# A decoder layer with 64 experts: a third buffer for the experts' gate and up weights, all weights on one queue

## What is computed

```python
gprob = jax.nn.softmax((hf @ w_rg) + b_rg, axis=-1)          # top 1 of 8 groups
elog = ...                                                    # top 2 of the group's 8 experts
def expert_block(args):
    xi, e = args
    return (jax.nn.silu(xi @ w_gate[e]) * (xi @ w_up[e])) @ w_down[e]
yb = lax.map(expert_block, (xb, block_expert)).reshape(R, D)
y = jax.ops.segment_sum(yb * slot_w[:, None], slot_tok, num_segments=T + 1)[:T]
```

## Time and profile before

| | |
|---|---|
| median of 3 runs | 1601.09 us (1597.41 to 1610.74) |
| the profiled execution's own time | 1600.42 us |
| its span, first to last instruction | 1598.7 us |
| TensorE busy | 1375.1 us (86%), granted clock 0.933 of full speed in the mean |
| VectorE, ScalarE, GpSimd busy | 827.9, 332.8, 245.4 us |
| moved by DMA | 277.85 MB, 174 GB/s in the mean |
| chain that ended last | PE 48%, DMA 21% (w_up alone 18%), DVE 19% |

### The profile page before, as it was taken

The page is one execution under the profiler, slowest core; times in us unless marked ns, Lnnn a source line. Parts: engine busy times, 40 slices in busy tenths (PEclk is TensorE's granted clock), DMA queues, the critical chain, the costliest instruction groups (busy, mean ns, idle before and its releaser), DMA issues.

```text
span 1598.7 us, 20949 instructions
## 1 busy us (share of the span) xinstructions
PE 1375.1 (86%) x6824; PEld 786.0 (49%) x6824; DVE 827.9 (52%) x1742; ACT 332.8 (21%) x901; POOL 245.4 (15%) x356
## 2 busy tenths in 40 slices
PE   5899999999999899999999698777887788877881
PEld 4548557575585665855847564532332232322330
DVE  1296685875857848668587323462223222222225
ACT  3123223232222322212323211101111111111112
POOL 2211121111210211012111100014111111111110
PEclk9999999999999999999999779778999899998996
DMA  8921030311202202103020440259999999999994
GB/s 193 162 54 41 28 94 2 80 40 28 69 25 61 61 25 56 40 28 94 0 54 19 169 131 40 101 232 405 414 416 402 418 403 397 413 398 414 386 372 185
DMA packets 126884, 277.85 MB, mean 174 GB/s; under 512 B 21500, under 2 KB 95158, under 8 KB 102134
## 3 DMA queue, kind: packets, MB, share of 16 engines
q1 hardware_dynamic: 103990, 196.21, 34.0%
q10 hardware_dynamic: 10704, 66.06, 11.3%
q0 software_dynamic: 12160, 15.19, 3.0%
HBM read 272.43 MB, written 30.62 MB: 190 GB/s over the span
## 4 chain that ended last, share of the span: by engine, by line
PE 48%; DMA 21%; DVE 19%; issue 7%; ACT 5%; ACTq 0%; DVEq 0%; SPq 0%; POOLq 0%; POOL 0%
DMA arena<-in_w_up 18%; PE PB L1505 10%; PE PB L1161 7%; DVE arena L1679 5%; PE PB L1155 5%; DVE arena L1651 4%; PE PB L1111 4%; PE PB L1429 4%; PE PB L1239 2%; PE PB L1267 2%; DMA arena<-in_w_gate 1%; PE PB L1132 1%; PE PB L1088 1%; PE PB L1361 1%; PE PB L1322 1%
## 5 line engine op out<-in xcount | busy, mean ns | idle before, releaser
L1505 PE MATMUL PB<-arena 128*64 128x512 f32 x1024 | 263.5, 663 | 79.9 <-DMA arena<-in_w_up 67.7
L1505 PEld LDWEIGHTS PB<-arena 128*64 128x64 f32 x1024 | 76.5, 151 | 239.4 <-issue 145.9
L2023 DVE TENSOR_SCALAR arena<-arena 128x256 f32<-128x256 f32 x32 | 9.4, 294 | 327.5 <-ACT arena L996 327.4
L1155 PE MATMUL PB<-arena 128*128 128x384 f32 x512 | 171.2, 488 | 6.5 <-DVE arena L1652 6.5
L1161 PE MATMUL PB<-arena 128*128 128x128 f32 x1280 | 167.6, 286 | 6.2 <-ACT arena L874 5.5
L1137 PE MATMUL PB<-arena 128*128 128x512 f32 x384 | 169.1, 596 | 0.0
L1161 PEld LDWEIGHTS PB<-arena 128*128 128x128 f32 x1280 | 157.0, 199 | 14.2 <-ACT arena L874 7.4
L935 ACT ACTIVATE arena<-PB 128x512 f32<-128x512 f32 (+3 forms) x116 | 60.0, 521 | 384.7 <-PE PB L1513 211.5
L1155 PEld LDWEIGHTS PB<-arena 128*128 128x128 f32 x512 | 95.4, 190 | 70.8 <-DVE arena L1652 7.6
L1525 PE MATMUL PB<-arena 128*64 128x512 f32 x512 | 118.4, 605 | 12.1 <-DMA arena<-in_w_down 11.6
L1137 PEld LDWEIGHTS PB<-arena 128*128 128x128 f32 x384 | 71.6, 190 | 88.0 <-issue 87.5
(11 more groups left out here) (436 smaller groups left out, 1991.5 us busy)
## 6 DMA issues: line engine op xcount, KB each, us to landing
arena<-in_w_gate SPq DMA_DIRECT2D x64, 1024.0 KB, 11.0
arena<-in_w_down SPq DMA_DIRECT2D x64, 1024.0 KB, 19.5
arena<-in_w_up ACTq DMA_DIRECT2D x60, 1024.0 KB, 13.9
arena<-in_w_in SPq DMA_DIRECT2D x58, 512.0 KB, 6.2
Sb<-in_state_dn SPq DMA_DIRECT2D x8, 512.0 KB, 4.1
out<-Sb POOLq DMA_DIRECT2D x8, 512.0 KB, 3.9
arena<-in_w_out SPq DMA_DIRECT2D x1, 4096.0 KB, 12.2
arena<-in_w_up SPq DMA_DIRECT2D x4, 1024.0 KB, 7.5
```

The lines of the kernel that those rows point to most:

```text
L1155: last = mm(gate_bank[(n + 1) % 2][0:R, 0:3 * P], hT[:, c, n * P:n * P + R], wrow[:, c, :, :].rearrange("p g k -> p (g k)"), start=c == 0, ...
L1505: last = mm(gu_bank[a][half[k], :], xT[:, a, c, half[k]], wgu[a][:, k, :, c, :], start=c == 0, stop=c == KC - 1)
```

## The change

Gate and up weights of a pair get a third buffer, `wgu2`, and pair j uses buffer j mod 3. To make room the arena grows by 1792 elements a partition, `wgu1` begins right behind ys instead of behind xr, and hb and hid (the silu's tiles) move into pT and sig, which only the mixer uses. `wgu2` lies over router scratch (rt, M and others), so its first load waits for `s_ov_done`; both buffers of down weights now end below it, in the place of the router's h2T, and are both loaded after `s_lg_ps`. All expert weights, the ups too, are asked for by SP. Since 2 and 3 buffers meet again after six pairs, the loops of SP and TensorE go over six pairs. The two semaphores of the result copies, s_ye_a and s_ye_v, become one, s_ye_done. The diff, cut:

```diff
-        wgu_at = 37632 - 2 * KC * 2 * FE
+        wgu_at = 39424 - 2 * KC * 2 * FE
         X = cut(2, D)
         xT = cut(2, KC, P)
-        hb = cut(2, FE)
-        hid = cut(2, FE)
+        hb = pT.rearrange("p (a b) k -> p a (b k)", a=2)
+        hid = sig.rearrange("p a g k -> p (a g k)")[:, 0:2 * FE].rearrange("p (a f) -> p a f", a=2)
         hidT = cut(2, FE // P, P)
         ys = cut(2, D)
         assert top[0] <= xr_end
-        top[0] = xr_end
         wgu1 = cut(2, 2, KC, FE)
         wdn = (cut(2, FE // P, D), cut(2, FE // P, D))
+        assert top[0] <= h2_end
+        wgu2 = cut(2, 2, KC, FE)
         assert top[0] <= wgu_at
         top[0] = wgu_at
-        wgu = (cut(2, 2, KC, FE), wgu1)
+        wgu = (cut(2, 2, KC, FE), wgu1, wgu2)
...
+        def pair6(it, r):
+            return it * 6 + r, it * 3 + r // 2, r % 2, it * 2 + r // 3, r % 3
+        def later6(it, r, k):
+            return pair6(it + (r + k) // 6, (r + k) % 6)
...
@@ block.sync
-            sp.wait_ge(s_y2_ps, NT)
+            sp.wait_ge(s_x2_done, NT)
             for k in range(2):
                 load_gate_up(1, k, 2 + k)
             sp.wait_ge(s_lg_ps, NT)
+            for a in range(2):
+                for k in range(2):
+                    load_down(a, k, 2 * a + k)
+            sp.dma_start(nfin, norm_final_w.partition_broadcast(P)).then_inc(s_fin_in, 16)
+            sp.wait_ge(s_ov_done, 1)
             for k in range(2):
-                load_down(0, k, k)
-            sp.dma_start(nfin, norm_final_w.partition_broadcast(P)).then_inc(s_fin_in, 16)
-            def gate_up_weights(it, a):
-                sp.wait_ge(s_gu_ps, 1 + it * 2 + a)
+                load_gate_up(2, k, 4 + k)
+            def gate_up_weights(it, r):
+                j, _, _, _, g = pair6(it, r)
+                sp.wait_ge(s_gu_ps, j)
                 for k in range(2):
-                    sp.dma_start(wgu[a][:, k, 0, :, :], w_gate[...]).then_inc(gu_in[a], 16)
-            def down_weights(it, a):
-                sp.wait_ge(s_dn_ps, 1 + it * 2 + a)
+                    load_gate_up(g, k, j * 2 + k)
+            def down_weights(it, r):
+                j, _, a, _, _ = pair6(it, r)
+                sp.wait_ge(s_dn_ps, 1 + j)
                 for k in range(2):
-                    load_down(a, k, it * 4 + (2 * a + k))
-            with sp.Fori(1, NPAIR // 2) as it:
-                gate_up_weights(it, 0)
-                sp.wait_ge(s_ov_done, 1)
-                down_weights(it - 1, 1)
-                gate_up_weights(it, 1)
-                down_weights(it, 0)
-            down_weights(NPAIR // 2 - 1, 1)
+                    load_down(a, k, j * 2 + k)
+            gate_up_weights(0, 3)
+            for r in range(2, 6):
+                gate_up_weights((r + 2) // 6, (r + 2) % 6)
+                down_weights(0, r)
+            with sp.Fori(1, NPAIR // 6) as it:
+                for r in range(6):
+                    gate_up_weights(it + (r + 2) // 6, (r + 2) % 6)
+                    down_weights(it, r)
+            for r in range(NPAIR % 6):
+                down_weights(NPAIR // 6, r)
...
@@ block.scalar
-            def up_weights(it, a):
-                j = it * 2 + a
-                act.wait_ge(s_gu_ps, 1 + j)
-                for k in range(2):
-                    act.dma_start(wgu[a][:, k, 1, :, :], w_up[...]).then_inc(gu_in[a], 16)
...
@@ block.tensor
             def gate_up(p, c0, c1):
+                j, _, a, i, g = p
                 if c0 == 0:
                     pe.wait_ge(s_xt_done, 1 + j * 2 + 2)
-                    pe.wait_ge(gu_in[a], it * 64 + 64)
+                    pe.wait_ge(gu_in[g], i * 64 + 64)
                 for c in range(c0, c1):
                     for k in range(2):
-                        last = mm(gu_bank[a][half[k], :], xT[:, a, c, half[k]], wgu[a][:, k, :, c, :], ...)
+                        last = mm(gu_bank[a][half[k], :], xT[:, a, c, half[k]], wgu[g][:, k, :, c, :], ...)
-            with pe.Fori(0, NPAIR // 2 - 1) as it:
-                for a in range(2):
-                    overlapped(it, a)
-            overlapped(NPAIR // 2 - 1, 0, turn=False)
+            with pe.Fori(0, NPAIR // 6) as it:
+                for r in range(6):
+                    overlapped(it, r)
+            overlapped(NPAIR // 6, 0, turn=False)
```

More of the change, by code:

```diff
@@ L211, in program @@
         h2T = cut(2, KC, P)
+        h2_end = top[0]
         brb = cut(72)
@@ L1032, in _ @@
                 follow(0, a)
-            with act.Fori(1, NPAIR // 2 - 2) as it:
+            with act.Fori(1, NPAIR // 2 - 1) as it:
                 for a in range(2):
                     follow(it, a)
[L1036 to L1039, removed]
+            follow(NPAIR // 2 - 1, 0, turn=False)
+            follow(NPAIR // 2 - 1, 1, nxt=False, turn=False)
             def further(it, a, k):
@@ L1496, in turn_x, with gate_up, turn_hid @@
                     last.then_inc(s_xt_ps, 1)
-            def gate_up(it, a, c0, c1):
-                j = it * 2 + a
+            def gate_up(p, c0, c1):
+                j, _, a, i, g = p
                 if c0 == 0:
                     pe.wait_ge(s_xt_done, 1 + j * 2 + 2)
-                    pe.wait_ge(gu_in[a], it * 64 + 64)
+                    pe.wait_ge(gu_in[g], i * 64 + 64)
                 for c in range(c0, c1):
                     for k in range(2):
-                        last = mm(gu_bank[a][half[k], :], xT[:, a, c, half[k]], wgu[a][:, k, :, c, :], start=c == 0, stop=c == KC - 1)
+                        last = mm(gu_bank[a][half[k], :], xT[:, a, c, half[k]], wgu[g][:, k, :, c, :], start=c == 0, stop=c == KC - 1)
                 if c1 == KC:
                     last.then_inc(s_gu_ps, 1)
-            def turn_hid(it, a):
-                j = it * 2 + a
+            def turn_hid(p):
+                j, _, a, _, _ = p
                 pe.wait_ge(s_hid_done, j + 1)
@@ L1514, in turn_hid, with down @@
                 last.then_inc(s_hT2_ps, 1)
-            def down(it, a):
-                j = it * 2 + a
+            def down(p):
+                j, i, a, _, _ = p
                 pe.wait_ge(s_hT2_done, j + 1)
-                pe.wait_ge(dn_in[a], it * 32 + 32)
-                pe.wait_ge(s_ye_a, 1 + j)
-                pe.wait_ge(s_ye_v, 1 + j)
+                pe.wait_ge(dn_in[a], i * 32 + 32)
+                pe.wait_ge(s_ye_done, 2 + 2 * j)
                 for q in range(2):
@@ L1527, in down, with overlapped @@
                 last.then_inc(s_dn_ps, 1)
[L1530 to L1533, removed]
+            def overlapped(it, r, turn=True):
+                gate_up(later6(it, r, 1), 0, KC // 2)
+                turn_hid(pair6(it, r))
+                gate_up(later6(it, r, 1), KC // 2, KC)
                 if turn:
[L1535 to L1540, removed]
-            with pe.Fori(0, NPAIR // 2 - 1) as it:
-                for a in range(2):
-                    overlapped(it, a)
-            overlapped(NPAIR // 2 - 1, 0, turn=False)
-            turn_hid(NPAIR // 2 - 1, 1)
-            down(NPAIR // 2 - 1, 1)
-            def further(it, a, k):
-                turn_x(it, a)
-                gate_up(it, a, 0, KC)
-                turn_hid(it, a)
-                down(it, a)
+                    turn_x(later6(it, r, 2))
+                down(pair6(it, r))
+            turn_x(pair6(0, 0))
+            gate_up(pair6(0, 0), 0, KC)
+            turn_x(pair6(0, 1))
+            with pe.Fori(0, NPAIR // 6) as it:
+                for r in range(6):
+                    overlapped(it, r)
+            overlapped(NPAIR // 6, 0, turn=False)
+            turn_hid(pair6(NPAIR // 6, 1))
+            down(pair6(NPAIR // 6, 1))
+            def further(it, a, k):
+                p = pair2(it, a)
+                turn_x(p)
+                gate_up(p, 0, KC)
+                turn_hid(p)
+                down(p)
             further_blocks(pe, further)
```

34 lines of the change are left out of this document (15 added, 19 removed).

## The result

The changed kernel takes 1621.8 us (median of 4 runs, 1617.9 to 1629.2) where the kernel before took 1602.2 beside it: a ratio of 1.012, 95% interval 1.009 to 1.015. It is slower by 1.2%, and outside the predicted range. Its profiled execution took 1617.9 us, with a span of 1616.1.

A forecast was written before the change was run, and what follows sets the result against it. The expert-pair stage was taken as bound by the bytes; the twelve microseconds gained from the dips were spent at the start (7.1 and 5.0), TensorE ending 0.5 us earlier, so about 1600 us, range 1588 to 1612.

The forecast's parts named there:

- the dips: Expert-pair loop: bandwidth dips are a queue run dry, a third buffer fills them; gain 10.6 us and another 1.5 or so.
- No window under 400 until 1540: Sign for the expert-pair stream: after the idle start, no bandwidth window under 400 GB/s until 1540.
- (B): Rival, expert-pair stream: dips not a dry queue or prefetch not real; mean rate stays 407, 11.2 us more, 1611; chance 0.18.
- The start: First pairs' loads: unmoved bytes put the stream 7.1 us behind at ov_done (overflow table done), itself 5.0 us later.
- The stream: Weight loads from 1084.8 to pair 29's down: 191.7 MB at 417 GB/s, 459.8 us, plus 1.2 and 0.9.
- the release: SP's wait for ov_done ahead of pair 2's gate and up loads: ends at 1083.2 instead of 1078.2.
- the sum: Whole kernel: span 1598.2, plus 1.7 for the profiled run and 0.7 for the median, 1600.6, say 1600.
- The tail: From the start of down 29: TensorE needs 19.2 us as before, no new wait; the 32.3 us behind untouched.
- what costs nothing: Side edits: ScalarE loses two DMA issues a pair (0.8 us), SP issues six loads, merged semaphore, moved tiles, unrolled loop: free.
- (C): Rival, SP's queue: one queue with POOL's rows carries less than two; at 402 GB/s 17.1 us more, 1618; chance 0.07.
- (D): Rival, stream and start: one queue carries 424 GB/s with rows, gather not held up; 7.7 and 5.0 less, 1588; chance 0.18.

The follow-up runs named there:

- e1: The changed kernel with indices out of bounds for 28 of 32 pairs' gathers and scatters, so their rows don't move: 1592.3 us, ratio 0.991.
- e2: The changed kernel with each expert's token rows spread over other partitions by a table of places, same bytes: 1609.5 us, ratio 1.003.
- e3: The kernel before, with its two buffers, and the token rows spread over other partitions by a table of places: 1592.7 us, ratio 0.991.
- e8: The changed kernel with each expert's token rows crowded on fewer partition groups, same bytes: 1671.4 us, ratio 1.041.
- e6: The changed kernel with only pair 1's down loads moved back behind pair 0's gate and up products: 1623.3 us, ratio 1.011.
- e4: The changed kernel with pair 2's gate and up loaded into pair 0's buffer, then pair 1's down, before the wait for ov_done: 1606.4 us, ratio 1.001.
- e5: The kernel before, two buffers and its own start, with the up weights also issued from SP's queue: 1608.0 us, ratio 1.003.

## Why the prediction was wrong

**The step that failed is "the dips".** It said that they are a queue run dry, that a third buffer should fill them, and that the stream then has 417 GB/s up to its end. They fell on the issue times, and SP's queue was in fact short of work there. But by e1, e2, e3, e8 and the increments TensorE waited for the slowest engine's share of a load, and for that engine the stream had no break. The queue ran dry for the engines that were ahead. The deeper queue was real, and it filled: the rate of 1100 to 1300 is its filling, 419 GB/s where the kernel before had 410, and none of it shortened a wait. "No window under 400 until 1540" held until 1315 (395) and broke for good from 1380. The forecast had 12.1 us gained there; from down 5 to down 29, 2.3 were lost.

What spoke against it stood in the prediction itself: at a DMA share of 0.76 in a dip most engines are busy, which a queue run dry doesn't explain. Rival (B) named it ("not all is idle there") and asked no further which engines were busy and with what.

**The start was sized nearly right.** ov_done came 4.9 us later, the prediction had 5.0, and e6 takes it back. In part that is luck: the 5.0 were for the gather alone, which lost 3.6 (nearer to the 3.3 that the prediction set beside its own number), and the other 1.3 were lost before and behind it. The bytes that hadn't moved were put at 7.1; together 12.1, measured 14.1 by down 5. At 16.31 us for the 6.29 MB of a pair, 3.0 MB are 7.8 us and not 7.1; the other 1.4 us are not settled. Since the dips gave nothing back, all of it stood: e4 shows that it is the loss but for 0.6 us.

**The stream** was to take 461.9 us from 1084.8 to down 29; it took 478.9 from 1085.9 (the issue at 1084.3 and the 1.6 to the first bytes). Counted the other way: 184.5 MB of weights are 29.3 pairs, at the measured 16.31 us 478. Of the 18.1 us by which down 29 came later than forecast, 17.0 are this term, mis-sized because it took the mean rate for the rate of a load; the other 1.1 are the release, in a run whose mixer ended 1.2 us later. The median lies 3.9 us above the profiled execution, where the sum had 0.7.

**The tail and what costs nothing** held. Down 29 to the end of down 31 took 19.3 us (19.2 forecast), and 32 us stood behind it. The two issues less on ScalarE, the six loads on SP and the unrolled loop show in no wait.

**The rivals.** (B) gave 1611 by its mean rate of 407, the nearest in kind: the dips were not cured. Its price was short, because it took the mean of the engines again. The time came out where (C) had put it, 1618 and more, but (C)'s mechanism is refuted: one queue keeps the pace within 0.04 us of two (e5), and the kernel after showed 418 to 420 with the rows in it. (D), 424, fell with it.

## What to carry to other kernels

A bandwidth that dips is not always for want of buffers, and a dip at the issue times is no proof of it: compare the time that a unit of work takes with the bytes of the busiest engine, not with the mean over 16, and see how far apart a load's 16 increments lie. Small rows that are gathered and scattered beside a stream cost by the engine on which they crowd; choose their partitions so that each engine gets the same number. And an edit that puts an early load behind a late semaphore can cost its full delay, as here, where the stream behind it had no slack to give it back.

## What the hardware showed that was not expected

- 0.26 MB of rows a pair beside 6.29 MB of weights cost 1.19 us of 16.31 when they lie on neighbouring partitions, 0.71 when spread, 2.69 when crowded (paces of after, e2 and e8 less that of e1).
- A core's engines moved 419 GB/s of weights and rows over 200 us (after, 1100 to 1300), with the weights from one queue. The windows between the dips of before, with two, had 415 to 418, but that is not the queues' doing: e3_before_spread has two as well and 416 to 420.
- The shares of a pair's two down loads landed up to 23 us apart (kernel after), against 4.6 us with no rows beside them (e1).
- Behind a long queue SP's issues grow from 0.44 us to 2.10, and to 5.07 for two. These rows of e6_down_late are its eleventh to fourteenth load after the release at 1087.02; about nine of 1 MiB were not yet moved by then, an estimate from the 420 GB/s of the stream:

```profile
1092.20 0.89 SPq L557 DMA_DIRECT2D arena<-in_w_gate  x1
1093.14 2.10 SPq L558 DMA_DIRECT2D arena<-in_w_up  x1
1095.28 5.07 SPq L561 DMA_DIRECT2D arena<-in_w_down  x2
```

That SP waits there for room in its queue is the likely reading and was not tested; nothing stands behind it but more loads.
